# Moving the normed input's two halves to an address 16 bytes past a multiple of 64

## The chip, the cores and the metric

The program runs on one core of one Trainium2 chip. The metric is the device time of one execution in microseconds (us). Three runs of the kernel before took 1584.97, 1585.01 and 1586.6 us; their median is 1585.01 us.

## The reference, cut to what matters

The reference is two transformer-like blocks, each over 512 tokens of width 1024, in float32. The part that matters here is the same in all its stages: the input is normed per token, and the normed input h is multiplied with wide weight matrices.

```
h = rms_norm(x, pre_mix_norm);  proj = h @ w_in             # 1024 x 6688
mix = concatenate([o_a, o_s]) @ w_out;  x = x + rms_norm(mix)
h = rms_norm(x, pre_ffn_norm);  u = causal_dwconv(h @ w_up) # 1024 x 5632
f = (silu(gate) * up) @ w_down; x = x + rms_norm(f)
...
h = modulate(rms_norm_2(x), shift, scale)
p = h @ w_in_2;  gates = sigmoid(h @ w_branch_gate)         # 1024 x 2048 each
merged = g_f * (y_four @ w_fo) + g_a * (y_attn @ w_ao)
h = modulate(rms_norm_2(x), shift, scale)
a = relu(h @ w1);  x = x + gate * ((a * a) @ w2)            # 1024 x 4096, 4096 x 1024
```

Between these products stand a gated delta rule, a state space scan, a Fourier mix and a neighbourhood attention, which work on smaller matrices.

## The kernel before

The four engines and the DMA queue each run a program written out by hand, and semaphores join them. There is no planner: the order of the code is the order of each engine.

**A float32 product as three.** A weight block of 128 x 1024 arrives in `w_raw`. ScalarE copies it into `w_high` (line 1598), which rounds it to the one-pass matmul format fp32r, and VectorE puts the remainder into `w_low` (line 2382). The left operand is split in the same manner. `products` (lines 787 to 789) then issues three matmuls into the same PSUM bank: high by high, high by low, low by high.

**The tensors of the change.** `HH` ("h_high") and `HL` ("h_low") hold the high and the low part of the normed input: 128 partitions, 8 blocks of 512 tokens each, 4 bytes an element, so 16,384 bytes per partition for each. They serve in several ways:

- As the moving operand, 512 columns wide, in `column_block` (lines 787 to 789): the first input projection, the up projection, four blocks of the second input projection, the gates, a part of the branch outputs, and the first blocks of the last MLP.
- As the moving operand, 256 columns wide, in `token_half` and in `part`. The latter multiplies pairs of blocks in seven products in place of eight, with sums of tokens. The token sums lie in tensors of their own, `token_sum` and `token_sums`.
- As the stationary operand, 128 columns at a time, in `row_part` (lines 1335 to 1337), where `w_high` and `w_low` (512 columns) move. Its blocks of the context take `last_low` and `context_low` as the stationary operand instead.
- As room for the last four weight blocks of a down projection (`HHW`, `HLW`), where they are the moving operand of 512 columns in `last_rows` (lines 843 to 845). One of the down projections takes `last_high` and `last_low` for this instead.

`row_block` (lines 830 to 832) moves `w_high` and `w_low` past `act_high` and `act_low` and does not touch the two tensors.

**Where things lie.** Tensors are laid out one after the other in each partition in the order of the code, each start rounded up to a multiple of 32 bytes. In the kernel before, `w_high`, `w_low`, `act_high`, `act_low`, `h_high` (byte 49,280) and `h_low` (byte 65,664) all start at a multiple of 64. `conv_params` has 720 bytes, so what follows it starts 32 bytes past a multiple of 64: `arena` (105,824) and with it `last_high`, `last_low`, `context_low`, `token_sum` and `token_sums`. All slices that matmuls take of these tensors are multiples of 64 bytes further on, so they keep the remainder of their tensor.

In the profile's names a matmul reads `acc<-moving,stationary`.

Of the kernel before, what the change touches and what calls it, by code (L numbers as in the profile page):

```python
# [9 lines left out]
F32R = mybir.dt.float32r  # L10
# [5 lines left out]
P = 128  # L16
T = 512
NT = T // P
D = 1024
KD = D // P  # L20
# [186 lines left out]
def program(nc, a, laid, cst, dft, gmod, gcum, gpad, gexp, moved, out):  # L207
# [9 lines left out]
    with ctx:  # L217
        def sb(name, shape, dt=F32):
            return ctx.enter_context(nc.sbuf_tensor(name, shape, dt))
# [10 lines left out]
        def sem(name):  # L230
            name = ended.get(name, (name, 0))[0]
            if name not in S:
                S[name] = ctx.enter_context(nc.semaphore(name))
            return S[name]
# [8 lines left out]
            pass  # L243
        AH = sb("act_high", [P, 4, 512], F32R)
        AL = sb("act_low", [P, 4, 512], F32R)
        HH = sb("h_high", [P, KD, T], F32R)
        HL = sb("h_low", [P, KD, T], F32R)
        with nc.sbuf_tensor("cond_wide", [P, KD + 1, 32], F32) as CDW:
            pass
        SH = sb("small_w_high", [P, KD, 32], F32R)  # L250
# [34 lines left out]
        def arena(at, *shape):  # L285
            v = A[:, at:at + int(np.prod(shape))]
            if len(shape) == 2:
                return v.rearrange("p (a b) -> p a b", b=shape[1])
            if len(shape) == 3:
                return v.rearrange("p (a b c) -> p a b c", b=shape[1], c=shape[2])  # L290
            return v

        IDN, UPR, ONE, NOT = (C1[:, k * P:(k + 1) * P] for k in range(4))
        IDLE = HL[:, KD - 1, 0:P].bitcast(F32)
        FT = arena(FT_, CH, T)
# [10 lines left out]
        GR = arena(GR_, D)  # L306
        HHW, HLW = (v[:, :, :].rearrange("p (m a) b -> p m (a b)", a=2) for v in (HH, HL))
        XH = FLW[:, 1:3, :].rearrange("p a b -> p (a b)").rearrange("p (k t) -> p k t", t=CTX)
# [160 lines left out]
        def conv_bank(n):  # L469

            return n % 4 if n < SS_N else [0, 1, 6, 7][n - SS_N] if n < SS_N + 4 else n % 2
# [100 lines left out]
        def tokens(i):  # L572

            if i < 3:
                both = TOK12[:, i - 1] if i else TOK0[:, :, :, :]
                return both[:, 0], both[:, 1]
            return HH[:, 0:4, 256:512], HL[:, 0:4, 256:512]

        def moving(i):

            if i in (0, 5, 6):
                k, tc = slice(0, 4) if i == 0 else slice(4, 8), slice(256, 512) if i == 6 else slice(0, 256)
                return HH[:, k, tc], HL[:, k, tc]
            return tokens([1, 2, 0, 3][i - 1])
# [198 lines left out]
        def _(pe):  # L783
            def products(out_, wh, wl, xh, xl, start, stop, skip=False):


                pe.matmul(out_, wh, xh, start=start, stop=False, skip_group_check=skip)  # L787
                pe.matmul(out_, wh, xl, start=False, stop=False, skip_group_check=skip)  # L788
                return pe.matmul(out_, wl, xh, start=False, stop=stop, skip_group_check=skip)  # L789
# [4 lines left out]
            def column_block(g, off, bank, xh, xl, n=T, first=None, between=None):  # L794
                split_ready(g, off)
                s = off % 2
                for k in range(KD):
                    if first is not None:
                        pe.wait_ge(sem("n_low"), first + k + 1)
                    c = slice(k * P, (k + 1) * P)  # L800
                    m = products(PS[:, bank, 0:n], WH[:, s, c], WL[:, s, c], xh[:, k, :], xl[:, k, :],
                                 k == 0, k == KD - 1)
                    if between is not None and k == 1:
                        between()
                m.then_inc(sem("w_used"), 1)

            def token_half(off, bank, half, ks):
# [3 lines left out]
                for k in ks:  # L811
                    c = slice(k * P, (k + 1) * P)
                    m = products(PS[:, bank, tc], WH[:, s, c], WL[:, s, c], HH[:, k, tc], HL[:, k, tc],
                                 k == 0, k == KD - 1)
# [95 lines left out]
            def conv(n):  # L910
# [3 lines left out]
                elif n > 3:  # L914
                    pe.wait_ge(sem("conv_step"), 3 * n - 3)
                column_block(0, CONV_N + n, conv_bank(n), HH, HL, first=0 if n == 0 else None,
                             between=turn_last if n == 0 else None)
# [4 lines left out]
            for k in range(0, KD, 4):  # L922
                for n, h in enumerate((HH, HL)):
                    for g in range(4):
# [2609 lines left out]
```

## Time and profile before

| | |
|---|---|
| median of the runs | 1585.01 us |
| the profiled execution | 1585.33 us |
| its span, first to last instruction | 1583.5 us |
| TensorE (PE) busy | 1561.7 us, 99% |
| its weight loads (PEld) busy | 1313.0 us, 83% |
| VectorE (DVE) busy | 1041.9 us, 66% |
| ScalarE (ACT) busy | 727.1 us, 46% |
| GpSimd (POOL) busy | 169.4 us, 11% |

The span is 1.8 us shorter than the execution's own time. A matmul's duration in the profile is longer than the distance from its start to the next one's, because matmuls are pipelined; busy time counts each moment once.

### The profile page before, as it was taken

To read this page: it belongs to the slowest core of one execution; us is meant where nothing else is said; L and a number is where in the kernel's file an instruction comes from. 1 tells how busy PE (TensorE), PEld (TensorE's weight loads), DVE (VectorE), ACT (ScalarE), POOL (GpSimd) and SP (SyncE) were. 2 spreads that over 40 slices of the span, in tenths; PEclk is the share of its full clock that TensorE was granted. 3 is DMA by queue.
4 is the path that set the end of the run, shared out by engine and by line. 5 is a ranking of instruction groups with operands and counts; after the bars stand their busy time and mean duration, and the time that the engine had idled before them with its cause. 6 is when DMAs were issued, how large, how long until landed. Compare 5 with 4: busy or idle time off the path is not lost.

```text
span 1583.5 us, 22557 instructions
## 1 busy us (share of the span) xinstructions
PE 1561.7 (99%) x8773; PEld 1313.0 (83%) x8773; DVE 1041.9 (66%) x1597; ACT 727.1 (46%) x1280; POOL 169.4 (11%) x191
## 2 busy tenths in 40 slices
PE   9999999999999999999999999999999999999998
PEld 7888878789887877788888788888888899998886
DVE  5688868947546777766534538665657898875554
ACT  5464456555334333344324445544444666643221
POOL 2012124501101000000000123311000000000000
PEclk9999999999999999999999999999999999999999
DMA  7365233211353986532324132231224143432232
GB/s 202 87 163 137 81 96 91 81 55 41 120 189 122 306 280 234 201 104 81 121 100 133 29 97 68 73 87 54 80 81 133 41 108 107 107 120 93 93 100 72
DMA packets 198581, 180.84 MB, mean 114 GB/s; under 512 B 6078, under 2 KB 178189, under 8 KB 195412
## 3 DMA queue, kind: packets, MB, share of 16 engines
q1 hardware_dynamic: 195056, 171.13, 35.4%
q10 hardware_dynamic: 2276, 6.95, 1.3%
q0 software_dynamic: 1152, 1.44, 0.5%
q8 instruction: 64, 1.05, 0.3%
q14 instruction: 33, 0.27, 0.1%
HBM read 175.15 MB, written 4.58 MB: 114 GB/s over the span
## 4 chain that ended last, share of the span: by engine, by line
PE 92%; DVE 4%; ACT 2%; issue 1%; DMA 0%; POOL 0%; ACTq 0%; DVEq 0%; POOLq 0%
PE acc L787 16%; PE acc L788 16%; PE acc L789 16%; PE acc L830 7%; PE acc L832 7%; PE acc L831 7%; PE acc L1335 2%; PE acc L845 2%; PE acc L1336 2%; PE acc L843 2%; PE acc L844 2%; PE acc L1337 2%; PE acc L1479 1%; PE acc L1463 1%; DVE w_low L2382 1%
## 5 line engine op out<-in xcount | busy, mean ns | idle before, releaser
L2382 DVE TENSOR_TENSOR w_low<-w_raw,w_high 128x1024 fp32r<-128x1024 f32 x202 | 249.9, 1239 | 365.4 <-ACT w_high L1598 364.9
L787 PE MATMUL acc<-h_high,w_high 128*128 128x512 f32 (+1 forms) x1164 | 439.6, 378 | 6.4 <-DVE masks L3251 1.8
L1598 ACT ACTIVATE w_high<-w_raw 128x1024 fp32r<-128x1024 f32 x194 | 205.7, 1061 | 500.3 <-PE acc L789 250.0
L789 PE MATMUL acc<-h_high,w_low 128*128 128x512 f32 (+1 forms) x1164 | 431.9, 371 | 0.0
L788 PE MATMUL acc<-h_low,w_high 128*128 128x512 f32 (+1 forms) x1164 | 431.6, 371 | 0.0
L787 PEld LDWEIGHTS acc<-h_high,w_high 128*128 128x128 f32 x1164 | 219.4, 188 | 52.8 <-issue 11.6
L789 PEld LDWEIGHTS acc<-h_high,w_low 128*128 128x128 f32 x1164 | 219.3, 188 | 38.4
L788 PEld LDWEIGHTS acc<-h_low,w_high 128*128 128x128 f32 x1164 | 219.5, 189 | 36.5 <-issue 1.2
L830 PE MATMUL acc<-w_high,act_high 128*128 128x512 f32 x496 | 193.4, 390 | 0.8 <-DVE arena L2908 0.6
L831 PE MATMUL acc<-w_low,act_high 128*128 128x512 f32 x496 | 193.0, 389 | 0.0
L832 PE MATMUL acc<-w_high,act_low 128*128 128x512 f32 x496 | 193.0, 389 | 0.0
L830 PEld LDWEIGHTS acc<-w_high,act_high 128*128 128x128 f32 x496 | 93.1, 188 | 21.0 <-DVE arena L2908 1.0
L832 PEld LDWEIGHTS acc<-w_high,act_low 128*128 128x128 f32 x496 | 93.1, 188 | 19.4
L831 PEld LDWEIGHTS acc<-w_low,act_high 128*128 128x128 f32 x496 | 93.1, 188 | 19.2
L2507 DVE SCALAR_TENSOR_TENSOR arena<-acc,conv_params,arena 128x511 f32<-128x511 f32 (+2 forms) x108 | 80.6, 746 | 2.5
L2899 DVE SCALAR_TENSOR_TENSOR arena<-acc,params,arena 128x511 f32<-128x511 f32 x88 | 65.6, 746 | 1.5
L2396 DVE TENSOR_TENSOR act_low<-arena,act_high 128x512 fp32r<-128x512 f32 x78 | 53.0, 684 | 10.9 <-ACT act_high L1606 10.9
L1606 ACT ACTIVATE act_high<-arena 128x512 fp32r<-128x512 f32 x76 | 46.7, 620 | 22.8 <-PE acc L832 19.1
L2388 DVE TENSOR_TENSOR w_raw<-w_raw,arena 128x1024 f32<-128x1024 f32 x40 | 48.7, 1217 | 0.0
L3342 POOL TENSOR_SCALAR small<-small 128x1 f32<-128x1 f32 x17 | 3.9, 230 | 383.6 <-ACT arena L1625 383.6
L2278 ACT ACTIVATE w_high<-w_raw 128x512 fp32r<-128x512 f32 x44 | 27.7, 630 | 28.2 <-PE acc L789 24.2
L1335 PE MATMUL acc<-w_high,h_high 128*128 128x512 f32 x96 | 37.7, 392 | 1.6 <-DVE h_low L2442 1.0
(453 smaller groups left out, 2519.8 us busy)
## 6 DMA issues: line engine op xcount, KB each, us to landing
w_raw<-w_in SPq DMA_DIRECT2D x68, 512.0 KB, 3.9
w_raw<-w_mlp SPq DMA_DIRECT2D x64, 512.0 KB, 4.1
w_raw<-w_up SPq DMA_DIRECT2D x44, 512.0 KB, 4.0
arena<-w_ada SPq DMA_DIRECT2D x13, 1024.0 KB, 7.8
w_raw<-w_out SPq DMA_DIRECT2D x24, 512.0 KB, 3.4
early<-w_ada SPq DMA_DIRECT2D x11, 1024.0 KB, 6.2
w_raw<-w_down SPq DMA_DIRECT2D x22, 512.0 KB, 3.4
w_raw<-w_branch_gate SPq DMA_DIRECT2D x16, 512.0 KB, 4.0
```

Of the source, the lines that this page charges most:

```text
L787: pe.matmul(out_, wh, xh, start=start, stop=False, skip_group_check=skip)
L788: pe.matmul(out_, wh, xl, start=False, stop=False, skip_group_check=skip)
L789: return pe.matmul(out_, wl, xh, start=False, stop=stop, skip_group_check=skip)
L830: pe.matmul(o, AH[:, r, tc], WH[:, s, fc], start=k_is_0, stop=False)
L831: pe.matmul(o, AH[:, r, tc], WL[:, s, fc], start=False, stop=False)
L832: m = pe.matmul(o, AL[:, r, tc], WH[:, s, fc], start=False, stop=False)
L1335: pe.matmul(o, xh, WH[:, n % 2, wc], start=k == 0, stop=False)
L1598: f(WH[:, off % 2, :], RAW[:, off % 4, :], ACT.Copy).then_inc(sem("w_high"), 1)
L2382: tt(WL[:, off % 2, :], RAW[:, off % 4, :], WH[:, off % 2, :].bitcast(F32), ALU.subtract).then_inc(sem("w_low"), 1)
L2396: tt(AL[:, r, :], src[:, 4 * g + j, :], AH[:, r, :].bitcast(F32), ALU.subtract)\
L2507: stt(tap(n)[:, lag:T], PS[:, conv_bank(n), 0:T - lag], CW[:, at:at + 1], tap(n)[:, lag:T], ALU.mult, ALU.add).then_inc(sem("conv_step"), 1)
L2899: stt(o, PS[:, ffn_bank(q, j), 0:T - lag], w, o, ALU.mult, ALU.add).then_inc(sem("ffn_step"), 1)
```

## The change

`h_high` and `h_low` become two views of one tensor `h_wide` that has 8 elements (32 bytes) more. The first view starts 4 elements (16 bytes) in, the second 16,384 bytes behind it. A tensor `h_rest` of 8 elements follows. Together that is 64 bytes more, so all that comes behind lies 64 bytes further on and keeps its remainder by 64. `h_high` and `h_low` now start at bytes 49,296 and 65,680, 16 past a multiple of 64. Each engine issues the same instructions in the same order as before; only addresses differ.

```
-        HH = sb("h_high", [P, KD, T], F32R)
-        HL = sb("h_low", [P, KD, T], F32R)
+        HWIDE = sb("h_wide", [P, 2 * KD * T + 8], F32R)
+        HH, HL = (HWIDE[:, at:at + KD * T].rearrange("p (k t) -> p k t", t=T) for at in (4, 4 + KD * T))
+        sb("h_rest", [P, 8])
```

## Rows read from the trace of the kernel before

**Rows 1.** The page: busy time, the granted clock in 40 slices, the chain's engines.

```profile
PE   1561.7 (99%) x8773; PEld 1313.0 (83%) x8773; DVE 1041.9 (66%) x1597; ACT 727.1 (46%) x1280; POOL 169.4 (11%) x191
...
PEclk9999999999999999999999999999999999999999
...
PE 92%; DVE 4%; ACT 2%; issue 1%; DMA 0%; POOL 0%; ACTq 0%; DVEq 0%; POOLq 0%
```

**Rows 2.** Waits of the span: engine line, whom for, us in total, times, longest.

```profile
PE acc L787 <- DVE masks L3251: 1.8, 1, 1.8
...
PE acc L787 <- DVE w_low L2382: 0.8, 2, 0.6
```

**Rows 3.** PE's groups, shapes kept apart: busy us, mean ns | idle before.

```profile
L787 PE MATMUL acc<-h_high,w_high 128*128 128x512 f32 x960 | 381.5, 397 | 1.9 <-DVE h_low L2409 1.1 <-DVE w_low L2382 0.8
...
L788 PE MATMUL acc<-h_low,w_high 128*128 128x512 f32 x960 | 373.9, 389 | 0.0
...
L844 PE MATMUL acc<-h_low,act_high 128*128 128x512 f32 x96 | 37.3, 389 | 0.0
...
L844 PE MATMUL acc<-last_low,act_high 128*128 128x512 f32 x32 | 12.7, 395 | 0.0
...
L1336 PE MATMUL acc<-w_low,h_high 128*128 128x512 f32 x96 | 37.4, 389 | 0.0
...
L1336 PE MATMUL acc<-w_low,last_low 128*128 128x512 f32 x32 | 12.6, 395 | 0.0
```

**Rows 4.** PE's timeline, lines 843 to 845: start us, duration us.

```profile
1214.12 0.40 PE L843 MATMUL acc<-last_high,act_high 128*128 128x512 f32 x1
...
1223.92 0.40 PE L843 MATMUL acc<-last_high,act_high 128*128 128x512 f32 x1
```

**Rows 5.** The same lines with the slices of h, near the span's end.

```profile
1565.81 0.39 PE L843 MATMUL acc<-h_high,act_high 128*128 128x512 f32 x1
...
1575.79 0.39 PE L845 MATMUL acc<-h_high,act_low 128*128 128x512 f32 x1
```

**Rows 6.** PE's groups of 256 columns, shapes kept apart.

```profile
L788 PE MATMUL acc<-h_low,w_high 128*128 128x256 f32 x204 | 57.7, 283 | 0.0
...
L788 PE MATMUL acc<-h_low,act_high 128*128 128x256 f32 x84 | 23.8, 283 | 0.0
...
L788 PE MATMUL acc<-token_sums,w_high 128*128 128x256 f32 x76 | 21.3, 281 | 0.0
```

**Rows 7.** PE's timeline in the pairs of the last MLP.

```profile
1282.75 0.28 PE L787 MATMUL acc<-h_high,act_high 128*128 128x256 f32 x1
...
1284.55 0.28 PE L787 MATMUL acc<-token_sums,w_high 128*128 128x256 f32 x1
...
1287.98 0.28 PE L789 MATMUL acc<-token_sum,w_low 128*128 128x256 f32 x1
```

**Rows 8.** PE's timeline after a wait in the same stage.

```profile
1268.91 0.28 PE L788 MATMUL acc<-h_low,w_high 128*128 128x256 f32 x1
...
1269.97 0.28 PE L788 MATMUL acc<-h_low,w_high 128*128 128x256 f32 x1
```

**Rows 9.** DVE's and ACT's groups that write h or the last blocks.

```profile
L2403 DVE TENSOR_TENSOR h_low<-w_raw,h_high 128x1024 fp32r<-128x1024 f32 x12 | 14.7, 1222 | 1.3 <-ACT h_high L1615 1.3
...
L2403 DVE TENSOR_TENSOR last_low<-w_raw,last_high 128x1024 fp32r<-128x1024 f32 x4 | 4.9, 1218 | 0.3 <-ACT last_high L1615 0.3
...
L1615 ACT ACTIVATE h_high<-w_raw 128x1024 fp32r<-128x1024 f32 x12 | 12.6, 1048 | 0.7 <-DVE w_raw L2388 0.7
...
L1615 ACT ACTIVATE last_high<-w_raw 128x1024 fp32r<-128x1024 f32 x4 | 4.2, 1055 | 0.8 <-DVE w_raw L2388 0.8
```

## The prediction, made before the changed kernel ran

> **What bounds the kernel now.** I read the page first. TensorE is busy 1561.7 of 1583.5 us, its granted clock is full in all 40 slices, and 92% of the chain that ended last is TensorE's [rows 1]. The list of waits comes next: TensorE's longest single wait is 1.8 us, and for the weights' low halves, the work that VectorE does all the time, it waits 0.8 us in all [rows 2]. So the kernel is a stream of matmuls laid end to end, and what changes the step from one start to the next changes the time almost one for one. At full clock, 2.4 GHz, 512 columns need 512 / 2.4 = 213.3 ns.
>
> The step has to be read off the timeline, since a matmul's duration (389 ns) overlaps its successor's. Lines 843 to 845 with the slices of h start 44 steps apart between 1565.81 and 1575.79: 9.98 / 44 = 226.8 ns a step [rows 5]. That is 13.5 ns above the columns' own time. A duration moves with the step, so a difference of two mean durations of one shape is a difference of steps.
>
> **What the change does, part by part.** No instruction comes, goes or moves. What changes is where three kinds of matmul read, and where VectorE and ScalarE write h.
>
> *Count.* Of 512 columns with h moving there are 960 x 3 (lines 787 to 789, one line of the three with its count in [rows 3]) and 96 x 3 (lines 843 to 845). With h stationary there are 96 x 3 (lines 1335 to 1337). That is 2880 + 288 + 288 = 3456. Of 256 columns with h moving there are (204 + 84) x 3 = 864 [rows 6].
>
> *Price with 512 columns.* No operand of a one-pass matmul lies 16 bytes past a multiple of 64 in the kernel before, so the price must be bounded by neighbours. The trace has the same line with an operand at 32 past: `last_high` and `last_low`. As the moving operand they take line 844 from a mean of 389 to 395 ns; as the stationary operand `last_low` takes line 1336 from 389 to 395 ns [rows 3]. The timeline says the same: 42 steps between 1214.12 and 1223.92, 9.80 / 42 = 233.3 ns [rows 4] against 226.8 [rows 5], 6.5 ns more. I take 6.3 ns, between the two readings. For 16 past, the bounds are: nothing at all, if a 16-byte shift is too small to matter; 12.6 ns, twice the row, if a start at 16 is worse placed than one at 32; and below nothing down to -13.5 ns, if the shift took away all that a step costs beyond its columns. I take the 32-byte row as it stands because it is the only row in which such an operand leaves the multiple of 64, and because it comes out equal in both roles, as if all that counts is that one of the two operands is off the 64-byte grid. 3456 x 6.3 ns = 21.8 us.
>
> *Price with 256 columns.* Here the row points the other way. Fifteen steps with h take 1282.75 to 1284.55, 120.0 ns each; the 29 steps after them with the token sums, which lie 32 past, take 3.43 us, 118.3 ns each [rows 7]. The mean durations agree, 283 against 281 ns [rows 6]. So 864 x -1.7 ns = -1.5 us.
>
> *Why the two signs go together.* Behind a wait the matmuls of 256 columns with h, still on the grid, also step by 118 ns: nine steps in 1.06 us [rows 8]. So there seem to be two rhythms in which weight load and matmul can follow each other, one with 226.8 and 120.0 ns and one with 233.3 and 118.3 ns. Operands on the grid settle into the first and shifted ones stay in the second. That is my reading for carrying the row of 32 over to 16: a shifted operand does not fall into the first rhythm.
>
> *VectorE and ScalarE.* The split of a 1024-wide block takes 1222 and 1048 ns into h and 1218 and 1055 ns into the last blocks at 32 past [rows 9]. Differences of -4 and +7 ns on a few dozen instructions are nothing, and TensorE's stream hides them: the two engines are 66% and 46% busy [rows 1]. If that cover were gone, some 40 instructions of 7 ns (40 is my estimate of all that write h) would cost 0.3 us.
>
> *What is hidden.* 8% of the chain is not TensorE's [rows 1]; matmuls that run beside those stretches get slower for free. Most of the stretches are hand-overs in which no h matmul runs, so I take 5% off, not 8%. No wait is added. The waits that TensorE has are mostly for results of its own matmuls and stay; the 0.8 us for the low halves may go.
>
> *Sum.* 21.8 - 1.5 = 20.3 us; less 5%, 19.3 us. The profiled execution took 1585.33 us (span 1583.5 and 1.8 around it), which gives 1604.6; it stood 0.3 us above the median of the runs, so I predict 1604.3 us. The term's own uncertainty (6.0 to 6.7 ns a step, 0 to 8% hidden) makes that 1601 to 1608.
>
> **The rivals.**
>
> *A shift of 16 bytes costs nothing (1585).* For it: both kinds of shift seen in the trace are of 32 bytes; nothing shows that smaller ones count. Against it: 32 bytes do count, and a grid finer than 32 that would forgive 16 would have forgiven 32 as well. Only a rule peculiar to 32 would leave 16 alone. The Trainium skill, "SBUF — State Buffer", on the cachelines under its section on the DMA port swizzle, speaks for this rival: it gives lines of 16 bytes, and by that a start at 16 past touches as many lines as one on the grid. By the same rule a start at 32 past would be free too, and there the trace disagrees, 233.3 against 226.8 ns; so I give the rule little.
>
> *The shift helps (1578, other side).* TensorE reads the moving operand and, for the next matmul, the stationary one at the same time. On the grid both start at the same place within 64 bytes, and the 13.5 ns above the columns' time might be what that meeting costs. 16 bytes apart they might miss each other. For it: with 256 columns a shift does save 1.7 ns. Against it: with 512 columns a shift of 32, which also sets them apart, costs 6.5. If all 3456 + 864 = 4320 matmuls saved 1.7 ns, it would be 7.3 us: 1577.7. It would decide from the point where the step with 512 columns is under 226 ns (3456 x 0.9 ns = 3 us). At the very end, all 13.5 ns gone, 46.7 us, 1538; I see no row that leads there. By the Trainium skill, "TensorE: Matmul & The Clock Gate", section "Wait — 56ns, not 53.3ns?", a warm matmul steps at its columns plus about 2.5 ns; at that, 512 columns would take 215.8 ns, and 11 x 3456 ns = 38 us would be to be had. The rows disagree for this format even on the grid.
>
> *The price goes with the distance (1595).* Half of 32 bytes, half of 6.3 ns: 3456 x 3.15 = 10.9, less 0.7 for the narrow ones, 10 us. For it, nothing but smoothness; against it, the trace shows two rhythms and not a scale.
>
> *16 is worse than 32 (1626).* Twice the price, 43.5 us less 1.5 and 5%, 40 us. The rows neither support nor exclude it.
>
> **How the numbers follow.** As at 32 past: 58%, 1604.3. Nothing: 17%, 1585. Helps: 13%, around 1578. Half: 8%, 1595. Double: 4%, 1626. A change of 0.2% (3 us) is about what a measurement of this kernel tells from none. Faster by more than that needs the third case, with a little from the noise of the second: 0.14. Within 0.2%: most of the second and the weak end of the third, 0.15. Slower: the rest, 0.71. The range runs from 1582 to 1611: it holds the likeliest, the case of nothing and the half, and leaves out most of the helping case and the double one. The likeliest case's own range is 1601 to 1608.
>
> **What the profile after would show.** If right: the groups of lines 787 and 788 with 512 columns at means about 6 ns above 397 and 389 [rows 3], the 288 of the down projections and the 288 of the second input projection at about 395, the 256-column groups at 281 instead of 283, the `w_high,act_high` groups and the `last_high` groups unchanged, TensorE's busy time up by 19 to 21 us and its idle time the same. A step in the timeline of 233 ns with h. If the means stay at 389, the shift of 16 is free and the first rival holds; if they fall, the second. If the means rise by 6 ns and the time by much less, my reading of what is hidden was wrong. If means of groups that do not touch h move, the cause is not where I look for it.

## The result, and the profile after

The changed kernel took 1596.34, 1596.73 and 1596.88 us: median 1596.73 against 1585.01, a ratio of 1.0068 with a 95% interval of [1.0051, 1.0084]. It is slower by 11.7 us. I had predicted slower and 1604.3 us, so the direction was right, the range held it, and the size was 19.3 where 11.7 came. The likeliest case's own range, 1601 to 1608, missed, and of the prices that I had listed the nearest is that of a rival to which I gave 8% (half the price, 1595).

The page of the changed kernel, its first row and the chain by engine, answers to [rows 1]. The profiled execution took 1596.73 us, its span 1594.9.

```profile
PE 1574.1 (99%) x8773; PEld 1312.5 (82%) x8773; DVE 1039.8 (65%) x1597; ACT 727.0 (46%) x1280; POOL 170.9 (11%) x191
...
PE 94%; DVE 3%; ACT 1%; issue 1%; DMA 0%; POOL 0%; DVEq 0%; ACTq 0%; POOLq 0%
```

TensorE's busy time grew by 1574.1 - 1561.7 = 12.4 us and the span by 11.4. VectorE and ScalarE did the same work in the same time. All of it is in TensorE's stream.

TensorE's groups with shapes kept apart (busy us, mean ns of one) answer to [rows 3] and [rows 6]. Line numbers are one higher than before, and both halves of h have the name `h_wide`.

```profile
L788 PE MATMUL acc<-h_wide,w_high 128*128 128x512 f32 x960 | 385.5, 402 | 1.9 <-DVE h_wide L2410 1.1 <-DVE w_low L2383 0.8
L790 PE MATMUL acc<-h_wide,w_low 128*128 128x512 f32 x960 | 378.3, 394 | 0.0
L789 PE MATMUL acc<-h_wide,w_high 128*128 128x512 f32 x960 | 378.3, 394 | 0.0
...
L832 PE MATMUL acc<-w_low,act_high 128*128 128x512 f32 x496 | 193.0, 389 | 0.0
...
L789 PE MATMUL acc<-h_wide,w_high 128*128 128x256 f32 x204 | 57.6, 282 | 0.0
...
L1337 PE MATMUL acc<-w_low,h_wide 128*128 128x512 f32 x96 | 37.9, 394 | 0.0
L845 PE MATMUL acc<-h_wide,act_high 128*128 128x512 f32 x96 | 37.8, 394 | 0.0
...
L789 PE MATMUL acc<-h_wide,act_high 128*128 128x256 f32 x84 | 23.4, 279 | 0.0
...
L789 PE MATMUL acc<-token_sums,w_high 128*128 128x256 f32 x76 | 21.2, 279 | 0.0
...
L1337 PE MATMUL acc<-w_low,last_low 128*128 128x512 f32 x32 | 12.7, 395 | 0.0
...
L845 PE MATMUL acc<-last_low,act_high 128*128 128x512 f32 x32 | 12.6, 395 | 0.0
```

Every group of 512 columns with h rose by 4 to 7 ns, in both roles; the groups without h stayed (389 for `w_low,act_high`, 395 for the last blocks). The narrow groups with h, of 256 columns, fell by 1 to 4 ns. Matmuls moved that do not touch h: the token sums went from 281 to 279 ns [rows 6]. The prediction had said that such a movement would put the cause elsewhere, and it was the first hint that the grid is not 64 bytes: `arena`, and the token sums in it, had moved by 64.

The timeline of the changed kernel (start us, duration us) shows the step, the time from one matmul's start to the next one's, as [rows 5] did. These two rows are 24 steps apart.

```profile
59.61 0.39 PE L788 MATMUL acc<-h_wide,w_high 128*128 128x512 f32 x1
...
65.17 0.39 PE L788 MATMUL acc<-h_wide,w_high 128*128 128x512 f32 x1
```

5.56 us / 24 = 231.7 ns, neither the 226.8 of the old place nor the 233.3 of 32 past. Starts read to the nanosecond repeat as 235, 230, 227, 234: four steps make 926 or 927 ns.

Not all of the difference between the two profiled executions comes from the addresses. In the one after, TensorE's granted clock fell from its full level of 2.4 GHz to the lower one, 1.2 GHz, for 3.4 us, just after a wait of 1.8 us for VectorE. The first row below is a stretch (start:end, us, TensorE's busy time, granted clock, DMA share, GB/s); the other two are 12 steps apart.

```profile
1281.40:1284.90 3.50, 3.50 (x18) 0.51 1.02 274
```

```profile
1281.81 0.41 PE L788 MATMUL acc<-h_wide,w_high 128*128 128x256 f32 x1
...
1284.37 0.41 PE L788 MATMUL acc<-h_wide,w_high 128*128 128x256 f32 x1
```

2.56 us / 12 = 213.3 ns a step where the neighbours take 116.7. Some 15 matmuls of 256 columns lost about 1.5 us in this way. The execution before has the same wait at 1268.7 and a granted clock of 1.00 behind it. So the mean durations of the narrow groups of 204 understate what the shift gives them: outside that stretch the step of all narrow matmuls with h went from 119.9 to 116.6 ns.

### The profile page after: what moved, and what is told of

Its sections match the earlier page's. It is cut to its first block, busy times and chain, and to the rows that moved or that the text cites. A ratio compares the mean times of both kernels' runs of the same rounds, so it can differ in the third digit from the quotient of the medians.

```text
span 1594.9 us, 22557 instructions
## 1 busy us (share of the span) xinstructions
PE 1574.1 (99%) x8773; PEld 1312.5 (82%) x8773; DVE 1039.8 (65%) x1597; ACT 727.0 (46%) x1280; POOL 170.9 (11%) x191
## 4 chain that ended last, share of the span: by engine, by line
PE 94%; DVE 3%; ACT 1%; issue 1%; DMA 0%; POOL 0%; DVEq 0%; ACTq 0%; POOLq 0%
PE acc L788 17%; PE acc L790 17%; PE acc L789 17%; PE acc L831 7%; PE acc L832 7%; PE acc L833 7%; PE acc L1336 2%; PE acc L845 2%; PE acc L1338 2%; PE acc L846 2%; PE acc L844 2%; PE acc L1337 2%; PE acc L1480 1%; PE acc L1464 1%; DVE early L2708 1%
## 5 line engine op out<-in xcount | busy, mean ns | idle before, releaser
L788 PE MATMUL acc<-h_wide,w_high 128*128 128x512 f32 (+1 forms) x1164 | 443.4, 381 | 6.4 <-DVE masks L3252 1.8
L789 PE MATMUL acc<-h_wide,w_high 128*128 128x512 f32 (+1 forms) x1164 | 435.9, 374 | 0.0
L790 PE MATMUL acc<-h_wide,w_low 128*128 128x512 f32 (+1 forms) x1164 | 435.8, 374 | 0.0
L788 PEld LDWEIGHTS acc<-h_wide,w_high 128*128 128x128 f32 x1164 | 219.6, 189 | 56.2 <-issue 12.5
L790 PEld LDWEIGHTS acc<-h_wide,w_low 128*128 128x128 f32 x1164 | 219.6, 189 | 41.9
L789 PEld LDWEIGHTS acc<-h_wide,w_high 128*128 128x128 f32 x1164 | 219.7, 189 | 40.2 <-issue 1.2
L833 PEld LDWEIGHTS acc<-w_high,act_low 128*128 128x128 f32 x496 | 93.1, 188 | 19.3
L1336 PE MATMUL acc<-w_high,h_wide 128*128 128x512 f32 x96 | 38.3, 399 | 1.6 <-DVE h_wide L2443 1.1
```

What stands on the lines that cost most here:

```text
L833: m = pe.matmul(o, AL[:, r, tc], WH[:, s, fc], start=False, stop=False)
L1336: pe.matmul(o, xh, WH[:, n % 2, wc], start=k == 0, stop=False)
```

## The experiments

Each run's own kernel before is its yardstick; those medians were 1585.27, 1585.32 and 1585.35 us.

**Sweep 1: pairs of places by themselves.** A small kernel that leaves out the computation and only issues matmuls. Its core:

```
for name, past in PAST.items():        # 0, 4, 8, 16, 32, 48 bytes
    mov[name] = sb("mov_" + name, [P, 528], F32R)[:, past // 4:past // 4 + 512]
...
m = pe.matmul(PS[:, i % 8, 0:n], sta[s_][:, c], mov[m_][:, 0:n], start=True, stop=True)
```

> This kernel leaves out the whole computation: it only runs 48 one-pass matmuls in a row for each of 28 pairs of places of the moving and the stationary operand, and stores one product. Read: the mean duration of each group (a duration moves one for one with the step). Theory A, the grid: any operand off the multiple of 64 costs, in either role. With 512 columns 389 ns at grid/grid; about 394 with the moving operand at 16 and at 48 past; 395 to 396 at 32 past, in either role; still 394 to 396 where both operands are 16 (or 32) past. Theory B, the distance between the two operands: 389 again where both are 16, or both 32, past. Theory C, the price grows with the bytes past: 4 and 8 past cost 1 to 3 ns, 16 past 5, 32 past 10, 48 past 15. With 256 columns A expects 283 on the grid and 279 to 282 off it; 384 columns on the grid 389 - 53 = 336.

It took 280.67 us. Some of its groups:

```profile
L65 PE MATMUL acc<-mov_past_fortyeight,sta_grid 128*128 128x512 f32 x48 | 11.5, 400 | 0.0
L65 PE MATMUL acc<-mov_past_thirtytwo,sta_grid 128*128 128x512 f32 x48 | 11.4, 396 | 0.0
...
L65 PE MATMUL acc<-mov_past_sixteen,sta_past_sixteen 128*128 128x512 f32 x48 | 11.4, 395 | 0.0
...
L65 PE MATMUL acc<-mov_past_sixteen,sta_past_fortyeight 128*128 128x512 f32 x48 | 11.0, 389 | 0.0
```

None of the three theories came out whole. Two operands that are both off any multiple of 64 ran at 389, and 16 with 16 at 395. The case of both on the grid, the x96 group, is spoilt by its cold start in the mean, but its second half steps at 232.2 ns on average, not 226.7. So a multiple of 64 for both operands is not enough. The sweep did not copy the kernel's distances between tensors, which turned out to be the point.

**h at 32 past.** `HH, HL` start at element 8 of `h_wide` in place of 4.

> Both halves of h at 32 past a multiple of 64, all else as in the changed kernel. Theory A (grid): a step of 233.3 ns as with the last blocks at 32, so against 16 past another 1.6 ns on 3300 matmuls, 5 us, less 0.5 for the narrow ones: 1601 to 1602 us. Theory C (price grows with the distance): twice what 16 past costs, 1608. If 16 past was special and 32 is as cheap: 1597.

Measured: 1601.53 us, ratio 1.0102 [1.0085, 1.0119]. One group:

```profile
L789 PE MATMUL acc<-h_wide,w_high 128*128 128x512 f32 x960 | 379.3, 395 | 0.0
```

The row that my prediction leaned on was right for 32 past: the expected 1601 to 1602 us came. The prediction's own sum, 19.3 us, would have been too high even there, where 16.3 us came.

**h at 48 past.** `HH, HL` start at element 12; the padding grows so that the rest keeps its remainder by 64.

> Both halves of h at 48 past. Theory A: 48 and 16 past are mirror images on a grid of 64, four steps until the pattern repeats, so the same time as 16 past, 1596 to 1597 us, mean durations of 394. Theory C: three times the price of 16 past, 1620. A grid of 32 or 16 bytes would give 1585 and is excluded by the changed kernel already.

Measured: 1601.52 us, 1.0101 [1.0084, 1.0118]. Theory A's mirror image is false: 48 costs as 32 does, not as 16. Theory C's 1620 is false too. The timeline has two rhythms with the same operands, on the same lines. The first two rows are 22 steps apart, the next two 18.

```profile
59.69 0.40 PE L790 MATMUL acc<-h_wide,w_low 128*128 128x512 f32 x1
...
64.82 0.40 PE L788 MATMUL acc<-h_wide,w_high 128*128 128x512 f32 x1
...
99.64 0.39 PE L789 MATMUL acc<-h_wide,w_high 128*128 128x512 f32 x1
...
103.78 0.39 PE L789 MATMUL acc<-h_wide,w_high 128*128 128x512 f32 x1
```

5.13 / 22 = 233.2 ns, and 4.14 / 18 = 230.0 ns. All slices of one tensor here have the same remainder by 256, so what the chain falls into is decided by something other than the addresses' remainders.

**h and w both at 16 past.** `w_high` and `w_low` become views of `w_wide` in the same manner:

```
+        WWIDE = sb("w_wide", [P, 4096 + 8], F32R)
+        WH, WL = (WWIDE[:, at:at + 2048].rearrange("p (s c) -> p s c", c=1024) for at in (4, 4 + 2048))
+        sb("w_rest", [P, 8])
```

> h and the weights' halves w_high and w_low all at 16 past; act_high and act_low stay on the grid. Theory A (grid): groups with h stay at 394, the 496 x 3 with w moving and act stationary rise from 389 to 394: 1597 + 1488 x 4.9 ns = 1604 us. Theory B (relative place): h with w at equal remainders falls back to 389, so does w moving with h stationary; only h with act (288) and w with act (1488) pay: 1585 + 1776 x 4.9 ns = 1594 us.

Measured: 1591.19 us, 1.0036 [1.0022, 1.005].

```profile
L790 PE MATMUL acc<-h_wide,w_wide 128*128 128x512 f32 x960 | 372.8, 388 | 0.0
...
L833 PE MATMUL acc<-w_wide,act_high 128*128 128x512 f32 x496 | 195.2, 394 | 0.0
...
L846 PE MATMUL acc<-h_wide,act_high 128*128 128x512 f32 x96 | 37.8, 394 | 0.0
```

h with w is back to 388, though both lie 16 past, while the act groups pay, though act lies on the grid. So the relation of the two addresses counts. Theory A is dead, theory B stands for now, and was 3 us too high.

One thing about this layout matters later. `w_rest` pushes all that follows 64 bytes further, so h lies at 80 past its place in the kernel before and w at 16: 64 bytes past the old distance. In a settled stretch the step is (65.57 - 60.13) / 24 = 226.7 ns:

```profile
60.13 0.39 PE L789 MATMUL acc<-h_wide,w_wide 128*128 128x512 f32 x1
...
65.57 0.39 PE L789 MATMUL acc<-h_wide,w_wide 128*128 128x512 f32 x1
```

**Sweep 2: the kernel's own triples, moved by some bytes.** The same order of matmuls, the same PSUM banks, and the kernel's distance of 32,768 bytes between w and h, plus an offset:

```
(wh, wl), (xh, xl) = weights(w_past, j, k), normed(h_past, k, n)
pe.matmul(PS[:, j, 0:n], wh, xh, **one)
pe.matmul(PS[:, j, 0:n], wh, xl, **two)
m = pe.matmul(PS[:, j, 0:n], wl, xh, **three)
```

> This kernel leaves out the whole computation: it runs 48 matmuls for each of 28 cases in the kernel's own order (three per block of k: weights high by h high, high by low, low by high, same PSUM bank, the kernel's own distance of 32,768 bytes between w and h), only moved by some bytes, one source line per matmul and case. Theory B64 (what counts is the distance between the moving and the stationary address modulo 64): mean durations of 389 for h at 0, 64, 80 - 16, 128, 256, 512, 1024 past, and for w and h both at 16 or both at 32; 394 at 16 and 80; 395 to 396 at 32, 48 and 96, also with w moved alone. Theory B-large (the same, modulo 128 or more): 64, 128, 256, 512 or 1024 past leaves 389 as well. Theory A (each operand's own grid): both at 16 stays at 394. 256 columns: 283 at 0 and 64, 279 to 281 at 16, 32, 48. The two last cases (banks in rotation; one moving block throughout) tell which of the two made the first sweep's grid case unsettled: 389 where it is not the cause, 394 or more where it is.

Groups of the middle matmul of the cases h 4, h 16, h 32, h 128, h 256 and h 512, with w at its old place:

```profile
L88 PE MATMUL acc<-h_wide,w_wide 128*128 128x512 f32 x16 | 6.4, 400 | 0.0
...
L100 PE MATMUL acc<-h_wide,w_wide 128*128 128x512 f32 x16 | 6.3, 394 | 0.0
...
L106 PE MATMUL acc<-h_wide,w_wide 128*128 128x512 f32 x16 | 6.3, 395 | 0.0
...
L136 PE MATMUL acc<-h_wide,w_wide 128*128 128x512 f32 x16 | 6.3, 394 | 0.0
L142 PE MATMUL acc<-h_wide,w_wide 128*128 128x512 f32 x16 | 6.2, 390 | 0.0
...
L148 PE MATMUL acc<-h_wide,w_wide 128*128 128x512 f32 x16 | 6.2, 389 | 0.0
```

Mean of the last 36 steps of each case (ns, 512 columns unless noted; "reversed" is the reversed sweep below, whose case of 256 columns at 64 came first and is spoilt by the cold start). "h further by" counts bytes past h's old place, with w at its own:

```
h further by      0     4     8    16    32    48    64    80    96   128   256   512  1024
step          226.7 237.9 233.3 231.7 233.3 230.0 228.9 231.1 233.3 232.4 226.7 226.7 226.7
256 columns   120.0             118.6 116.7 118.3 117.8
reversed 512  226.7 237.7 233.3 231.7 233.3 233.3 228.9 231.1 233.3 233.3 226.7 226.7 226.7
reversed 256  120.0             116.7 116.7 118.3
```

The cases with w moved as well (512 columns; the distance is what h - w adds to the old one, modulo 256):

```
h, w      0, 16  16, 16  32, 32  16, 48  48, 16   0, 32   0, 48
distance    240       0       0     224      32     224     208
step      226.7   230.0   226.7   226.7   233.3   233.3   233.3
reversed  233.3   231.1   226.7   226.7   232.2   233.3   233.3
```

With w at its old place only 0, 256, 512 and 1024 give 226.7. So theory B64 is false and B-large holds for these, with 256 bytes; I had not named that number, since my list of expectations for 256 to 1024 allowed either. Rotating the PSUM banks or repeating one moving block changed nothing (226.7 both). In sweep 1 the two grid tiles were 12,672 bytes apart, which is 128 past a multiple of 256, and its 232.2 ns is this table's 232.4. Its pairs at distances of 8, 80 and 96 agree too (233.3, 231.1, 233.3 ns); the one at 16, with the stationary tile at 48, does not: 228.3 ns against 231.7.

The second table shows that the distance alone does not settle the step. h at 16 with w at 48, and h at 0 with w at 32, have the same distance by 256, and step at 226.7 and 233.3 ns, in both orders of the cases. Their middle matmuls in the sweep, in this order:

```profile
L178 PE MATMUL acc<-h_wide,w_wide 128*128 128x512 f32 x16 | 6.2, 389 | 0.0
...
L190 PE MATMUL acc<-h_wide,w_wide 128*128 128x512 f32 x16 | 6.3, 396 | 0.0
```

And both at 16 are a multiple of 256 apart, yet step at 230.0 and 231.1.

**h 64 bytes further, whole.** `sb("h_front", [P, 16])` ahead of `h_high`: every operand keeps its remainder by 64.

> h as in the kernel before, 64 bytes further on. Theory A and B64: nothing changes, 1585 us, means of 389. Theory B-large: the distance between w and h is no longer a multiple of 128, so some or all of the 4.9 to 6.5 ns on 3300 matmuls come back: 1596 to 1602.

Measured: 1587.14 us, 1.0014 [1.0004, 1.0024]; the step of the 512-column matmuls with h, averaged over the trace, is 229.5 ns. In a settled stretch it is (65.27 - 59.78) / 24 = 228.8:

```profile
59.78 0.39 PE L788 MATMUL acc<-h_high,w_high 128*128 128x512 f32 x1
...
65.27 0.39 PE L788 MATMUL acc<-h_high,w_high 128*128 128x512 f32 x1
```

Two of the groups:

```profile
L789 PE MATMUL acc<-h_low,w_high 128*128 128x512 f32 x960 | 376.5, 392 | 0.0
...
L1337 PE MATMUL acc<-w_low,h_high 128*128 128x512 f32 x96 | 38.0, 395 | 0.0
```

Slower, though nothing that matmuls read left its remainder by 64. The step fits the sweep's 228.9; my 1596 was drawn from 16 past and too high. By the mean step the 3456 matmuls pay 2.2 ns each, 7.6 us; the narrow ones with h and the token sums give 2.6 us back. That leaves 5 us where the median rose by 1.8; the rest was not traced. With h and w both at 16, the distance was the same 64 bytes past the old one, and the settled step 226.7 ns: once more two places with one distance and two steps.

**Only h_high at 16 past.**

```
-        HH = sb("h_high", [P, KD, T], F32R)
+        HWIDE = sb("h_high_wide", [P, KD * T + 8], F32R)
+        HH = HWIDE[:, 4:4 + KD * T].rearrange("p (k t) -> p k t", t=T)
+        sb("h_rest", [P, 8])
```

> Only h_high at 16 past; h_low on the grid. If each matmul pays for its own operands, two thirds of the price: 1585 + 8 = 1593 us, with the middle one of the three (h_low) back near 389. If the rhythm of the whole chain is what is lost, the middle one pays as well and the time is that of the full change, 1597.

Measured: 1593.87 us, 1.0056 [1.0039, 1.0072].

```profile
L789 PE MATMUL acc<-h_high_wide,w_high 128*128 128x512 f32 x960 | 388.1, 404 | 1.9 <-DVE h_low L2411 1.1 <-DVE w_low L2384 0.8
L790 PE MATMUL acc<-h_low,w_high 128*128 128x512 f32 x960 | 377.6, 393 | 0.0
L791 PE MATMUL acc<-h_high_wide,w_low 128*128 128x512 f32 x960 | 375.4, 391 | 0.0
```

Inconclusive. The time came out near the two-thirds figure. The first of the three is at 404, above the 402 of the full change, and the middle one, whose own operand is on the grid of 64, did not come back to 389. But in this kernel `h_low` also lies 64 further than before, which gives 392 by itself (the run above). The settled step over all three is 231.1 ns; if each paid for its own place, it would be (231.7 + 228.9 + 231.7) / 3 = 230.8, and if the whole chain paid for 16 past, 231.7. So this run does not tell whether a matmul pays for its own operands alone.

**h 256 bytes further.** `sb("h_front", [P, 64])` ahead of `h_high`.

> h as in the kernel before, 256 bytes further on. Theory D (by the second sweep: the step is set by the distance between the two addresses modulo 256): nothing changes, 1585 us, means of 389 for lines 788 to 790, and the 256-column groups back at 283. Rival E (only the exact old distance of 32,768 bytes, or a larger power of two, gives 389): 1587 to 1601 us.

Measured: 1585.71 us, 0.9999 [0.999, 1.0008]; `h_low,w_high` with 512 columns at 389 again, so theory D holds for h moved by itself. One part seemed to miss: the narrow groups of 204 came out at 286, not 283.

```profile
L789 PE MATMUL acc<-h_low,w_high 128*128 128x512 f32 x960 | 373.9, 389 | 0.0
...
L789 PE MATMUL acc<-h_low,w_high 128*128 128x256 f32 x204 | 58.4, 286 | 0.0
```

The place is not the reason. Away from stretches such as the next one their step is 119.9 ns, as in the kernel before. Here the granted clock was at the lower level, 1.2 GHz, after a wait of 1.8 us for VectorE, and 15 of these matmuls stepped at 213 ns, about 1.5 us more in all:

```profile
1269.05:1272.55 3.50, 3.50 (x19) 0.51 1.03 279
```

**h 4 bytes past.** `HH, HL` start at element 1.

> Both halves of h only 4 bytes past the old place. Theory D with the second sweep's table (a step of 237.9 ns at 4 past against 226.7): some 10.6 ns more on 3300 to 3456 matmuls, 35 us, 1618 to 1621 us, means of 399 to 401. Theory C (price grows with the bytes): a quarter of what 16 past costs, 3 us, 1588.

Measured: 1618.63 us, 1.0209 [1.0193, 1.0224], within the 1618 to 1621 that the sweep's table gave. The smallest shift is the dearest.

```profile
L789 PE MATMUL acc<-h_wide,w_high 128*128 128x512 f32 x960 | 383.6, 400 | 0.0
...
L845 PE MATMUL acc<-h_wide,act_high 128*128 128x512 f32 x96 | 38.3, 399 | 0.0
```

**A version that uses it.**

```
-        WH = sb("w_high", [P, 2, 1024], F32R)
-        WL = sb("w_low", [P, 2, 1024], F32R)
+        WHW = sb("w_high", [P, 2, 64 + 1024], F32R)
+        WLW = sb("w_low", [P, 2, 64 + 1024], F32R)
+        WH, WL = WHW[:, :, 64:1088], WLW[:, :, 64:1088]
...
+        sb("arena_pad", [P, 8])
...
-                c = slice(at % 2 * 512, at % 2 * 512 + 512)
-                return WH[:, at // 2, c], WL[:, at // 2, c]
+                c = slice(56 + at % 2 * 512, 56 + at % 2 * 512 + 512)
+                return WHW[:, at // 2, c], WLW[:, at // 2, c]
```

> A version drawn from the sweep: arena is moved by 32 bytes, so that last_high, last_low and context_low lie a multiple of 256 from their partners (their 192 matmuls from 395 to 389: -1.3 us); in the pairs of the last MLP the weight ring's slots in w_high and w_low begin 32 bytes lower, so h and the token sums lie 32 bytes past them (420 matmuls with h from 120.0 to 116.7 ns, -1.4 us; 348 with token sums from 118.3 to 116.7, -0.6 us; the 156 with the ring's act slots +0.3). Theory D: 1582.3 us, a ratio of 0.998. If the ring's change of distance at every third part upsets the rhythm: 1584 to 1586.

Measured over five rounds: 1582.42 us, 0.9979 [0.997, 0.9988], 2.9 us faster than the kernel before and 14.3 faster than the changed one.

```profile
L790 PE MATMUL acc<-h_low,w_high 128*128 128x256 f32 x204 | 57.2, 280 | 0.0
...
L1338 PE MATMUL acc<-w_low,last_low 128*128 128x512 f32 x32 | 12.5, 389 | 0.0
...
L846 PE MATMUL acc<-last_low,act_high 128*128 128x512 f32 x32 | 12.5, 389 | 0.0
```

The last blocks fell from 395 [rows 3] to 389 and the narrow ones with h from 283 [rows 6] to 280, in a group that also holds the 192 matmuls outside the pairs, which the version does not touch.

**Sweep 2 in reverse order.** The same 26 cases, last first; the two with other banks and one moving block stay at the end.

> The second sweep with its 26 cases in reverse order (the whole computation is left out). If the step is a property of the two addresses alone, each case repeats its mean: 226.7 ns at 0, 256, 512, 1024, 231.7 at 16, 233.3 at 32, 230.0 at 48, 228.9 at 64. If it depends on the rhythm in which the chain came in, some cases change: I expect that of h 48 (230.0 in the sweep, 233.3 over most of the kernel with h at 48 past) and of w and h both 16 past.

The lines "reversed" of the tables above: with w at its old place all multiples of 256 repeat 226.7, most others repeat too, but h 48 went from 230.0 to 233.3 and 128 from 232.4 to 233.3, and with 256 columns h 16 from 118.6 to 116.7. Of the cases with w moved, w at 16 with h at 0 went from 226.7 to 233.3, w and h both at 16 from 230.0 to 231.1, and h 48 with w 16 from 233.3 to 232.2. The group rows of w 16 with h 0, of the sweep and of the reversed sweep:

```profile
L160 PE MATMUL acc<-h_wide,w_wide 128*128 128x512 f32 x16 | 6.2, 389 | 0.0
```

```profile
L142 PE MATMUL acc<-h_wide,w_wide 128*128 128x512 f32 x16 | 6.3, 394 | 0.0
```

So for some places the step depends on the rhythm in which the chain came in. For a distance of a multiple of 256 it did so only where both operands were 16 past.

A duration does not always move with the step, either: for h at 64 the middle matmul took 394 ns in the sweep and 388 in the reversed one, at a step of 228.9 in both. The mean over all three lines, or better the step itself, is what to read.

## Why the prediction was right in sign and too high in size

**What bounds the kernel: right.** The step of the matmul stream decides; the nine timed kernels moved the way their steps did.

**The count, 3456 and 864: right.** All those groups moved and, the token sums aside, no other large one by more than 2 ns.

**The price with 512 columns: the step that failed.** I put 6.3 ns on each of 3456, 21.8 us. The busy times of the groups with h (lines 788 to 790, 844 to 846, 1336 to 1338) grew by 15.4 us in sum, 4.5 ns each. Two parts. First, 16 past gives 231.7 ns and not 233.3: carrying the row of 32 over to 16 was the assumption. It would have been nearer at 32 and 48 (1601.5, 16 us more where the sum says 19.3). That is 1.6 ns, 5.5 us. Second, I took the settled 226.8 as what every matmul of before paid. It does not: after a switch of operands or a wait the stream of before also runs for some steps in a slower rhythm. The timeline of the kernel before shows it behind matmuls of another shape, 8 steps in 1.85 us, 231 ns each:

```profile
1066.31 0.39 PE L788 MATMUL acc<-h_low,w_high 128*128 128x512 f32 x1
...
1068.16 0.39 PE L787 MATMUL acc<-h_high,w_high 128*128 128x512 f32 x1
```

Averaged over all switches and waits before matmuls of h with w, the first nine steps take 228 to 233 ns each before 226.7 sets in. Over the trace of before the mean step of these matmuls is 227.3, not 226.7, which takes off 0.6 x 3456 = 2 us. The two come to 7.5 us; 1 us of it the prediction had already left out by taking 6.3 ns where the settled steps differ by 6.6. That leaves the 6.4 us between 21.8 and 15.4.

**The price with 256 columns: right in sum by luck.** -1.5 us predicted, -1.7 in the busy time of the groups with h. But the step at the full clock fell by 3.3 ns, from 119.9 to 116.6, and not by 1.7: that is -2.9 us, of which the stretch at the lower clock took back some 1.5. The token sums gave another 0.8 that I had not counted, since I took them for untouched. They lay 32 bytes short of a multiple of 256 from the weights, and are now 32 past it.

**Two rhythms: half right.** Waits and switches do leave the chain in another rhythm, and h at 16, 32 or 48 past alone keeps it out of the 226.7 one. But there are more than two (226.7, 228.9, 230.0, 231.7, 233.3, 237.9), and what decides is not each operand's own multiple of 64. "All that counts is that one of the two operands is off the 64-byte grid" is wrong: both may be off it and run at 388 (h and w at 16), and both may be on it and still run slower (h 64 further).

**What is hidden: about right.** 5% predicted; 12.4 us of busy time became 11.4 us of span, 8%. The stretch at the lower clock, 1.5 us, is larger than the 1 us on which this share rests, so the share is rough.

**The rivals.** "Costs nothing" is excluded; the 16-byte lines of the Trainium skill, "SBUF — State Buffer", on the cachelines under its section on the DMA port swizzle, by which a shift by whole lines changes nothing, would have made 16, 32, 48 and 64 further all free, and all four measured slower (1.0014 to 1.0102). "The price goes with the distance" has the nearest time, 1595 against 1596.7, and that is luck: its reason is excluded by 4 bytes being dearest and by 48 costing what 32 does. "16 is worse than 32" is excluded by 1596.7 against 1601.5 (its own sum comes to 1625, not 1626). "Helps" was wrong for 16 past as a whole, but its idea, that the two reads disturb each other through their relative place, is nearer to what the runs show than my own: moving either operand alone by 32 bytes gave 233.3 ns, moving both gave 226.7.

## What to carry to other kernels

In a stream of one-pass float32 matmuls in which each loads new weights, look at the step between starts, and at the distance between the moving and the stationary address. For 512 columns a multiple of 256 bytes was the safe choice here, as long as the two were not both 16 past their old places. With 256 columns 32 bytes past it was best (116.7 against 120.0 ns in the sweeps; 117.7 in the kernel with h at 32 past). Moving an operand by a padding in front of it cost between nothing and 2% here though no instruction changed; compare groups that were not touched, since they show where the distance moved with them. A row from a neighbouring offset gave the sign, but not the size. Read steps along with mean durations, and the granted clock of the same stretch: 15 matmuls at the lower clock moved a group of 204 by 3 ns.

## What the runs showed that I had not expected

- With w at its place, the step depends on how far h is from it modulo 256 bytes: 226.7 ns at 0, 256, 512 and 1024; 228.9 to 237.9 ns at nine other distances between 4 and 128 (two of them, 48 and 128, changed with the order of the cases).
- The distance is not all. With the same distance by 256, h at 16 and w at 48 stepped at 226.7 and h at 0 and w at 32 at 233.3 ns; h and w both at 16 stepped at 230.0 or 231.1, where the old places give 226.7; and 64 past the old distance gave 228.9 with w at its place and 226.7 with w 16 further. What the rule in both addresses is stays open.
- In units of 16 columns at the full clock (6.67 ns), the steps are 34 at a multiple of 256 (226.7), 34.75 at 16 past (231.7), 34.5 and 35 at 48 past (230.0, 233.3), 35 at 32 past (233.3), and with 256 columns 18 (120.0) and 17.5 (116.7). So one, two or four of these steps together make a whole number of 16-column (64-byte) pieces; 228.9 and 231.1 need three, and 232.4 and 237.9 fit no such small number. That the weight load and the moving read take turns in such pieces is my reading and was not shown; nor is it known why the period is 256 bytes.
- The same addresses can hold two rhythms (h at 48 past: 233.2 and 230.0 ns in one run; w at 16: 226.7 or 233.3 ns by the case that ran before). What selects one at a switch stays open.
- The granted clock can fall to 1.2 GHz for 3.4 us after a wait of 1.8 us in one execution and not in another at the same wait; what decides it was not tested.
